# Layer norms of a two-layer encoder run tile by tile instead of side by side

## Chip, cores and metric

One core of a Trainium2 chip runs the whole program in one launch. The metric is the device time of one execution in microseconds (us), as the median over several runs. The engines are named as in the profile: PE is TensorE's matmul side and PEld its weight load, DVE is VectorE, ACT is ScalarE, POOL is GpSimd, SP is SyncE, which here only issues DMAs.

## What is computed

The reference is a float32 encoder of two layers over one sequence of 256 tokens and a model width of 1024. Each layer has four sub-blocks, each followed by a residual sum and a layer norm:

```
alpha = (2 * DEPTH) ** 0.25
x = LN(alpha*x + 0.5 * swiglu(x))          n = 0
x = LN(alpha*x + hybrid_mix(x))            n = 1
x = LN(alpha*x + cross_attention(x, mem))  n = 2
x = LN(alpha*x + 0.5 * swiglu(x))          n = 3
LN(v): (v - mean(v)) * rsqrt(mean((v - mean(v))**2) + 1e-5) * g + b
```

## The kernel before

**Tiles.** The 256 tokens are two token tiles (t = 0 and 1) of 128 partitions. X holds both, 128x1024 each. A matmul operand is split into a high and a low part in a reduced format, and three matmuls make one product (lines 412 to 414). So every weight block ("unit") is loaded to RAW by SP, copied by ACT to WH (the high part, line 917), and DVE subtracts to get WL (the low part, line 1232); ten units per two layers have this subtraction on POOL instead (line 1768). RAW, WH and WL are rings of three. The transposed activations XH and XL are made the same way: PE transposes X to PSUM (turn_x, line 481), ACT copies to XH, DVE subtracts to XL (both called turned).

**Order.** Each engine has its own program, written out by hand, and the engines meet only in semaphores. A loop runs over the two layers (l). After each sub-block comes boundary(l, n) on DVE and on ACT; the last norm of a layer (n = 3) is written out after ffn(l, 1).

**The norm on DVE.** norm_center(t) makes the residual sum of one tile with its row sum (line 1268), the negative mean (L1271), and XG, the centred row times the gain (L1274). It waits for the first token tile's product (y_half) at t = 0 and for the whole product (unit_used) at t = 1. ACT squares the centred row meanwhile and sums it (square, line 937). norm_scale(a, b) turns the sums of tiles a to b-1 into the variance (L1281), takes the reciprocal root by two integer steps and three Newton rounds of three instructions (rsqrt, lines 1246 to 1251; 11 instructions on 128 x (b-a) elements), and then makes the final X of each tile (L1285), which lets PE transpose it. link() around a small instruction makes the next one wait for its result.

**What stands behind it in the queues.** ACT's boundary is: square tile 0, [at n = 2 one weight copy], square tile 1, [at n = 0 the copy of unit U_DQ+1, at n = 0 and 1 the copy of one bank of keys or values, kv_out], then the copies to XH. At n = 3 ACT goes on with ffn of the next layer: one weight copy, then the copies to XH. PE at n = 0 transposes tile 0, multiplies it by U_DQ, transposes tile 1, then needs U_DQ+1, whose low part POOL makes at the end of its queue of table work. PE at n = 1 transposes both tiles and only starts the product with U_WQ when both are turned. At n = 2 and at the next layer's ffn it works on tile 0 before tile 1 is transposed. After the last norm SP writes X to memory, one DMA for each token tile as each is ready.

Of the kernel before, what the change touches and what calls it, by code (L numbers as in the profile page):

```python
# [69 lines left out]
TWO_PI = 6.2831850  # L70


DVE_LINKS, POOL_LINKS = 224, 111


def build(nc, x_in, mem_in, wg, wu, wd, ln_g, ln_b, w_in, w_out, wq, wkv, wo, par, const, out):
# [12 lines left out]
    with ctx:  # L89
# [1130 lines left out]
        def _(dve):  # L1220
# [4 lines left out]
            def link(ins):  # L1225

                count["n"] += 1
                ins.then_inc(dve_link.sem, 1)
                dve.wait_ge(dve_link.sem, dve_link.at(layer["l"], count["n"]))
# [4 lines left out]
            def split(l, u, j=0, half=False):  # L1234
                s = u % RING
                n = 1024 if half else 2048
                if u in (U_DQ + 2, U_K[3], U_WQ + 1, U_FFN[1] + 2):

                    dve.wait_ge(split_lo.sem, split_lo.at(l, u))
                dve.wait_ge(split_hi.sem, split_hi.at(l, u + 1 + 3 * j))  # L1240
                low(WL[s][:, 0:n], RAW[s][:, 0:n], WH[s][:, 0:n]).then_inc(split_lo.sem, 1)

            def rsqrt(dst, src, n, work, done=None):

                a, b = SM[:, work:work + n], SM[:, work + n:work + 2 * n]
                link(v.tensor_scalar(b.bitcast(I32), src.bitcast(I32), 1, None, ALU.logical_shift_right))
                link(v.tensor_scalar(dst.bitcast(I32), b.bitcast(I32), -1.0, 1597463007.0, ALU.mult, ALU.add))
                for i in range(3):
                    link(v.scalar_tensor_tensor(a, dst, -0.5, dst, ALU.mult, ALU.mult))
                    link(v.tensor_tensor(a, a, src, ALU.mult))  # L1250
                    ins = v.scalar_tensor_tensor(dst, a, 1.5, dst, ALU.add, ALU.mult)  # L1251
                    if i < 2 or done is None:
                        link(ins)
                    else:
                        ins.then_inc(done.sem, 1)
# [4 lines left out]
            def norm_center(l, n, t, last_unit):  # L1260

                c = (0.5 if n in (0, 3) else 1.0) / ALPHA
                if t == 0:
                    dve.wait_ge(y_half.sem, y_half.at(l, n + 1))
                    dve.wait_ge(gb_in.sem, gb_in.at(l, 32 * (n + 1)))
                else:
                    dve.wait_ge(unit_used.sem, unit_used.at(l, last_unit + 1))
                v.scalar_tensor_tensor(X[:, t, :], Y[:, t, :], c, X[:, t, :], ALU.mult, ALU.add,
                                       accum_out=SM[:, 16 + t:17 + t]).then_inc(ln_sum.sem, 1)
                dve.wait_ge(ln_sum.sem, ln_sum.at(l, TT * n + t + 1))  # L1270
                v.tensor_scalar(SM[:, 18 + t:19 + t], SM[:, 16 + t:17 + t], -1.0 / D, None, ALU.mult)\  # L1271
                    .then_inc(ln_mean.sem, 1)
                dve.wait_ge(ln_mean.sem, ln_mean.at(l, TT * n + t + 1))
                v.scalar_tensor_tensor(XG[:, t, :], X[:, t, :], SM[:, 18 + t:19 + t], LNGB[:, 0, :],  # L1274
                                       ALU.add, ALU.mult).then_inc(ln_center.sem, 1)

            def norm_scale(l, n, a, b):

                dve.wait_ge(ln_square.sem, ln_square.at(l, TT * n + b))
                var = SM[:, 20 + a:20 + b]  # L1280
                link(v.tensor_scalar(var, var, 1.0 / D, EPS / ALPHA ** 2, ALU.mult, ALU.add))  # L1281
                rsqrt(SM[:, 22 + a:22 + b], var, b - a, 48)
                dve.wait_ge(ln_center.sem, ln_center.at(l, TT * n + b))
                for t in range(a, b):
                    v.scalar_tensor_tensor(X[:, t, :], XG[:, t, :], SM[:, 22 + t:23 + t], LNGB[:, 1, :],  # L1285
                                           ALU.mult, ALU.add).then_inc(x_ready.sem, 1)

            def turned(l, n, t):
                for half in range(2):
                    dve.wait_ge(xT_hi.sem, xT_hi.at(l, 4 * n + 2 * t + half + 1))  # L1290
                    cs = slice(4 * half, 4 * half + 4)
                    low(XL[:, cs, t * P:t * P + P], PS[:, 4 + 2 * t + half, :].rearrange("p (c n) -> p c n", c=4),
                        XH[:, cs, t * P:t * P + P]).then_inc(xT_lo.sem, 1)

            def boundary(l, n, last_u):
                norm_center(l, n, 0, last_u)
                if n == 2:

                    norm_scale(l, n, 0, 1)
                norm_center(l, n, 1, last_u)  # L1300
                if n < 2:
                    norm_scale(l, n, 0, 2)
                turned(l, n + 1, 0)
                if n == 2:
                    norm_scale(l, n, 1, 2)
                turned(l, n + 1, 1)
                if n == 1:
                    split(l, U_WQ + 1)
                if n > 0:
                    split(l, U_WQ + 2 if n == 1 else U_FFN[1] + 2)  # L1310
# [5 lines left out]
            def ffn(l, s):  # L1316
                b = U_FFN[s]
                if s == 0:
                    split(l, b)
                    turned(l, 0, 0)  # L1320
                    split(l, b + 1)
                    turned(l, 0, 1)
                    split(l, b + 2)
                h_mul(l, 22 * s + 1, 0)
                split(l, b + 3)
                h_mul(l, 22 * s + 1, 1)
                split(l, b + 4)

                def step(j, jj, last):
                    dve.wait_ge(hT_hi.sem, hT_hi.at(l, jj + (11 * s + 1)))  # L1330
                    low(HL[:, :, :], PS[:, 6, :].rearrange("p (c n) -> p c n", c=2), HH[:, :, :])\
                        .then_inc(hT_lo.sem, 1)
                    split(l, b + 5, jj)
                    h_mul(l, jj * 2 + (22 * s + 3), 0)
                    h_mul(l, jj * 2 + (22 * s + 3), 1)
                    if not last:
                        split(l, b + 6, jj)
                        split(l, b + 7, jj)

                step(0, 0, False)  # L1340
                if s == 0:
                    prepare_first(l)
                step(1, 1, False)
                if s == 0:
                    prepare_phase(l)
                step(2, 2, False)
                if s == 0:
                    prepare_rest(l)
                with dve.Fori(3, BLOCKS - 2) as j:
                    step(j, j, False)  # L1350
                step(BLOCKS - 2, BLOCKS - 2, True)
                if s == 0:
                    split(l, U_K[0])
                dve.wait_ge(hT_hi.sem, hT_hi.at(l, 11 * s + BLOCKS))
                low(HL2[:, :, :], PS[:, 6, :].rearrange("p (c n) -> p c n", c=2), HH2[:, :, :]).then_inc(hT_lo.sem, 1)
# [372 lines left out]
            with dve.Fori(0, DEPTH) as l:  # L1728
                layer["l"] = l
                v.memset(CIN[:, :, 0:3], 0.0).then_inc(cin_zero.sem, 1)  # L1730
                ffn(l, 0)
                split(l, U_DQ)
                boundary(l, 0, U_FFN[0] + 32)
                mix(l)
                boundary(l, 1, U_WOUT[4])
                xattn(l)
                boundary(l, 2, U_WO + 4)
                ffn(l, 1)
                norm_center(l, 3, 0, U_FFN[1] + 32)
                norm_center(l, 3, 1, U_FFN[1] + 32)  # L1740
                norm_scale(l, 3, 0, 2)
            assert count["n"] == DVE_LINKS, count["n"]


# [229 lines left out]
```

## Time and profile before

| | |
|---|---|
| time, median of 3 runs | 1393.96 us (1392.83 to 1393.98) |
| span of the profiled execution, first to last instruction | 1392.3 us |
| median less that span | 1.7 us |
| PE busy / PEld busy | 91% / 75% |
| DVE / ACT / POOL busy | 61% / 42% / 31% |
| granted TensorE clock, mean | 0.949 |

The profiled execution has no time of its own beside the span; what lies around the span is taken as the 1.7 us by which the median exceeds it. A busy PE is not a PE at its peak, because matmuls are pipelined; gaps of PE are what is to be looked for. The norms lie, in layer 0, from about 207 us (n = 0), 414 us (n = 1), 488 us (n = 2) and 689 us (n = 3); in layer 1 from about 893, 1103, 1177 and 1379 us.

### The profile page before, as it was taken

Reading aid. Unit: us, or ns where it says so; the run is one execution under the profiler, and the core shown is the slowest. Engines: PE = TensorE matmul, PEld = TensorE weight load, DVE = VectorE, ACT = ScalarE, POOL = GpSimd, SP = SyncE. Lnnn points to the kernel's source line nnn. Section 1 sums busy time; section 2 is a strip of 40 time slices with the busy share of each in tenths; the row PEclk is TensorE's granted clock in tenths of the full one; section 3 lists DMA queues with packets and bytes.
Section 4 is the critical chain, followed back from the end, with each engine's and each line's share of the span. In section 5 each row is a group of like instructions: output and inputs, shape, how many; then the busy total and the mean of one; then the engine's idle time right before and its main releaser. Section 6 shows DMA issues by size and latency. Waiting matters only on the chain.

```text
span 1392.3 us, 18724 instructions
## 1 busy us (share of the span) xinstructions
PE 1267.4 (91%) x6160; PEld 1048.2 (75%) x6160; DVE 854.8 (61%) x1208; ACT 581.8 (42%) x651; POOL 432.1 (31%) x331
## 2 busy tenths in 40 slices
PE   5999997979968979999889999889797899799996
PEld 5878886857758868888768788777576687688885
DVE  4675555697885574444566655628978746644554
ACT  5433344423633443444354343444255334344432
POOL 0028886386040010000000588853851200100000
PEclk8999999998999989999989999989799899899999
DMA  7755553323334335555355555433233343455550
GB/s 271 263 177 194 181 182 113 129 93 106 136 121 152 121 131 202 191 193 187 123 205 193 186 194 192 152 121 118 94 122 121 121 152 122 151 181 190 194 188 31
DMA packets 151435, 219.13 MB, mean 157 GB/s; under 512 B 6721, under 2 KB 119489, under 8 KB 151105
## 3 DMA queue, kind: packets, MB, share of 16 engines
q1 hardware_dynamic: 148352, 205.61, 43.5%
q0 software_dynamic: 2736, 11.59, 2.3%
q10 hardware_dynamic: 272, 1.05, 0.2%
q8 instruction: 34, 0.56, 0.2%
q14 instruction: 41, 0.33, 0.1%
HBM read 217.17 MB, written 1.05 MB: 157 GB/s over the span
## 4 chain that ended last, share of the span: by engine, by line
PE 50%; POOL 22%; issue 14%; DVE 11%; ACT 1%; POOLq 1%; DMA 1%; DVEq 0%; SPq 0%; ACTq 0%
PE PS L412 15%; PE PS L413 15%; PE PS L414 15%; POOL ESN L1783 2%; POOL EC L1788 2%; POOL EC L1786 2%; DVE SM L1251 2%; POOL EF L1781 2%; POOL EF L1787 1%; POOL ESN L1790 1%; POOL ESN L1779 1%; POOL ESN L1782 1%; POOL EF L1789 1%; POOL ZX L1841 1%; DVE XG L1274 1%
## 5 line engine op out<-in xcount | busy, mean ns | idle before, releaser
L1232 DVE TENSOR_TENSOR WL<-RAW,WH 128x2048 fp32r<-128x2048 f32 (+1 forms) x188 | 427.2, 2273 | 277.8 <-ACT WH L917 274.6
L917 ACT ACTIVATE WH<-RAW 128x2048 fp32r<-128x2048 f32 (+1 forms) x198 | 371.1, 1877 | 185.6 <-PE PS L414 185.4
L412 PE MATMUL PS<-WH,XH 128*128 128x512 f32 x832 | 339.1, 408 | 36.9 <-DVE XL L1232 20.3
L413 PE MATMUL PS<-WL,XH 128*128 128x512 f32 x832 | 332.2, 399 | 0.0
L414 PE MATMUL PS<-WH,XL 128*128 128x512 f32 x832 | 331.8, 399 | 0.0
L412 PEld LDWEIGHTS PS<-WH,XH 128*128 128x128 f32 x832 | 161.2, 194 | 75.1 <-issue 24.4
L414 PEld LDWEIGHTS PS<-WH,XL 128*128 128x128 f32 x832 | 161.1, 194 | 35.1
L413 PEld LDWEIGHTS PS<-WL,XH 128*128 128x128 f32 x832 | 161.7, 194 | 32.3
L412 PE MATMUL PS<-WH,HH 128*128 128x512 f32 x352 | 137.5, 391 | 2.4 <-DVE HL L1232 2.4
L414 PE MATMUL PS<-WH,HL 128*128 128x512 f32 x352 | 137.0, 389 | 0.0
L413 PE MATMUL PS<-WL,HH 128*128 128x512 f32 x352 | 137.0, 389 | 0.0
L1768 POOL TENSOR_TENSOR WL<-RAW,WH 128x2048 fp32r<-128x2048 f32 x10 | 45.7, 4568 | 171.0 <-ACT WH L917 171.0
L917 ACT ACTIVATE HH<-PS 128x512 fp32r<-128x512 f32 x44 | 26.3, 598 | 157.5 <-PE PS L443 156.9
L1232 DVE TENSOR_TENSOR HL<-PS,HH 128x512 fp32r<-128x512 f32 x44 | 30.4, 691 | 83.0 <-ACT HH L917 82.8
L982 ACT ACTIVATE SG<-PS 128x256 f32<-128x256 f32 x88 | 33.8, 384 | 108.7 <-PE PS L414 108.7
L412 PEld LDWEIGHTS PS<-WH,HH 128*128 128x128 f32 x352 | 66.1, 188 | 16.8 <-issue 3.2
L414 PEld LDWEIGHTS PS<-WH,HL 128*128 128x128 f32 x352 | 66.1, 188 | 13.7
L413 PEld LDWEIGHTS PS<-WL,HH 128*128 128x128 f32 x352 | 66.1, 188 | 13.6
L1874 POOL DMA_DIRECT2D PAR<-in_params x2 | 1.1, 534 | 228.3 <-PE PS L414 228.3
L412 PE MATMUL PS<-XH,WH 128*128 128x256 f32 x224 | 66.3, 296 | 3.2 <-DVE XL L1232 3.2
L413 PE MATMUL PS<-XL,WH 128*128 128x256 f32 x224 | 64.8, 289 | 0.0
L414 PE MATMUL PS<-XH,WL 128*128 128x256 f32 x224 | 64.8, 289 | 0.0
(280 smaller groups left out, 1990.6 us busy)
## 6 DMA issues: line engine op xcount, KB each, us to landing
RAW<-in_ffn_w_gate SPq DMA_DIRECT2D x88, 512.0 KB, 3.7
RAW<-in_ffn_w_up SPq DMA_DIRECT2D x88, 512.0 KB, 4.7
RAW<-in_ffn_w_down SPq DMA_DIRECT2D x88, 512.0 KB, 3.9
RAW<-in_w_in SPq DMA_DIRECT2D x44, 512.0 KB, 4.1
RAW<-in_xattn_wkv SPq DMA_DIRECT2D x32, 512.0 KB, 4.1
RAW<-in_xattn_wq SPq DMA_DIRECT2D x16, 512.0 KB, 3.9
RAW<-in_w_out SPq DMA_DIRECT2D x12, 512.0 KB, 3.6
RAW<-in_xattn_wo SPq DMA_DIRECT2D x12, 512.0 KB, 4.0
```

Source lines behind the costliest of these rows:

```text
L412: nc.tensor.matmul(out_ap, sh, mh, start=first, stop=False)
L413: nc.tensor.matmul(out_ap, sh, ml, start=False, stop=False)
L414: return nc.tensor.matmul(out_ap, sl, mh, start=False, stop=last)
L917: return nc.scalar.activation(dst, src, ACT.Copy)
L982: nc.scalar.activation(SG[:, t, :], PS[:, 4 + t, 0:FB], ACT.Silu).then_inc(sg_done.sem, 1)
L1232: return v.tensor_tensor(dst, full, hi.bitcast(F32), ALU.subtract)
L1251: ins = v.scalar_tensor_tensor(dst, a, 1.5, dst, ALU.add, ALU.mult)
L1768: g.tensor_tensor(WL[s][:, :], RAW[s][:, :], WH[s][:, :].bitcast(F32), ALU.subtract)\
L1781: link(g.tensor_scalar(EF[:, :], s, MAGIC, MAGIC, ALU.add, ALU.subtract))
L1783: link(g.tensor_tensor(s, s, c, ALU.add))
L1786: link(g.tensor_scalar(c, s, 0.25, None, ALU.add))
L1788: link(g.tensor_tensor(c, c, EF[:, :], ALU.subtract))
```

## The change

The norms at n = 0, 1 and 3 get the order that n = 2 has: tile 0's sum, centring, variance, reciprocal root and scale are all done before tile 1's residual sum begins, and tile 1 gets a reciprocal root of its own. At n = 0 and 1 the low parts of tile 0's transposed activations (turned) are made between tile 1's centring and its scale. Nothing changes at n = 2. ACT's, PE's, POOL's and SP's programs stay as they are.

```diff
-DVE_LINKS, POOL_LINKS = 224, 111
+DVE_LINKS, POOL_LINKS = 260, 111
...
             def boundary(l, n, last_u):
                 norm_center(l, n, 0, last_u)
-                if n == 2:
-
-                    norm_scale(l, n, 0, 1)
+                norm_scale(l, n, 0, 1)
                 norm_center(l, n, 1, last_u)
-                if n < 2:
-                    norm_scale(l, n, 0, 2)
                 turned(l, n + 1, 0)
-                if n == 2:
-                    norm_scale(l, n, 1, 2)
+                norm_scale(l, n, 1, 2)
                 turned(l, n + 1, 1)
...
                 ffn(l, 1)
                 norm_center(l, 3, 0, U_FFN[1] + 32)
+                norm_scale(l, 3, 0, 1)
                 norm_center(l, 3, 1, U_FFN[1] + 32)
-                norm_scale(l, 3, 0, 2)
+                norm_scale(l, 3, 1, 2)
```

DVE_LINKS counts the linked instructions of one layer: 12 more for each of the three norms.

## Rows read from the trace of the kernel before

**Rows 1.** The page, part 4: shares of the chain that ended last.

```profile
PE 50%; POOL 22%; issue 14%; DVE 11%; ACT 1%; POOLq 1%; DMA 1%; DVEq 0%; SPq 0%; ACTq 0%
```

**Rows 2.** Timeline of DVE, last norm: start us, busy us, instruction, tiles.

```profile
1378.57 1.23 DVE L1268 SCALAR_TENSOR_TENSOR X<-PS,X 128x1024 f32<-128x1024 f32 x1 [4.24 <-PE PS L414]
...
1381.23 1.22 DVE L1268 SCALAR_TENSOR_TENSOR X<-PS,X 128x1024 f32<-128x1024 f32 x1
...
1383.95 0.17 DVE L1281 TENSOR_SCALAR SM<-SM 128x2 f32<-128x2 f32 x1
...
1386.32 2.48 DVE L1285 SCALAR_TENSOR_TENSOR X<-XG,SM,LNGB 128x1024 f32<-128x1024 f32 x2
```

**Rows 3.** Timeline of DVE and POOL, norm n = 2 of layer 0.

```profile
490.95 0.15 DVE L1281 TENSOR_SCALAR SM<-SM 128x1 f32<-128x1 f32 x1
...
493.03 4.50 POOL L1768 TENSOR_TENSOR WL<-RAW,WH 128x2048 fp32r<-128x2048 f32 x1 [64.84 <-ACT WH L917]
...
493.07 4.47 DVE L1251 SCALAR_TENSOR_TENSOR SM<-SM 128x1 f32<-128x1 f32 x1
...
498.78 1.22 DVE L1268 SCALAR_TENSOR_TENSOR X<-PS,X 128x1024 f32<-128x1024 f32 x1
...
503.19 0.14 DVE L1281 TENSOR_SCALAR SM<-SM 128x1 f32<-128x1 f32 x1
```

**Rows 4.** Timeline of SP's queue at the end: the two output DMAs.

```profile
1387.64 1.54 SPq L401 DMA_DIRECT2D out<-X  x2
```

**Rows 5.** Timeline of ACT, DVE and PE, n = 3 of layer 0.

```profile
697.28 1.91 ACT L917 ACTIVATE WH<-RAW 128x2048 fp32r<-128x2048 f32 x1
...
700.19 2.29 DVE L1232 TENSOR_TENSOR WL<-RAW,WH 128x2048 fp32r<-128x2048 f32 x1
...
702.40 1.28 DVE L1232 TENSOR_TENSOR XL<-PS,XH 128x512 fp32r<-128x512 f32 x2
...
703.93 0.79 PE L412 MATMUL PS<-WH,XH 128*128 128x512 f32 x1 [3.67 <-DVE XL L1232]
```

**Rows 6.** Timeline of POOL, DVE, ACT and PE, n = 1 of layer 0.

```profile
412.94 4.62 POOL L1768 TENSOR_TENSOR WL<-RAW,WH 128x2048 fp32r<-128x2048 f32 x1 [13.34 <-ACT WH L917]
...
415.04 3.60 DVE L1274 SCALAR_TENSOR_TENSOR XG<-X,SM,LNGB 128x1024 f32<-128x1024 f32 x1
...
421.96 0.60 ACT L917 ACTIVATE KT<-PS 128x512 f32<-128x512 f32 x1 [0.71 <-PE PS L414]
...
423.92 2.48 DVE L1285 SCALAR_TENSOR_TENSOR X<-XG,SM,LNGB 128x1024 f32<-128x1024 f32 x2
...
429.87 0.58 PE L412 MATMUL PS<-XH,WH 128*128 128x256 f32 x1 [1.59 <-DVE XL L1232]
```

**Rows 7.** Timeline of DVE, POOL and PE, n = 0 of layer 0.

```profile
207.31 1.22 DVE L1268 SCALAR_TENSOR_TENSOR X<-PS,X 128x1024 f32<-128x1024 f32 x1
...
216.36 1.07 POOL L1789 TENSOR_SCALAR EF<-ESN 128x256 f32<-128x256 f32 x1 [0.19 <-POOL EC L1788]
...
216.42 3.08 DVE L1285 SCALAR_TENSOR_TENSOR X<-XG,SM,LNGB 128x1024 f32<-128x1024 f32 x2
...
218.38 1.59 POOL L1804 TENSOR_TENSOR CP<-PAR,CUR 128x256 f32<-128x256 f32 x1
...
225.20 4.54 POOL L1768 TENSOR_TENSOR WL<-RAW,WH 128x2048 fp32r<-128x2048 f32 x1
...
225.81 1.04 PE L481 MATMUL PS<-kst,X 128*128 128x128 f32 x8
...
229.79 0.50 PE L412 MATMUL PS<-WH,XH 128*128 128x512 f32 x1 [2.94 <-POOL WL L1768]
```

**Rows 8.** Windows: length, busy us (count) of PE, PEld, DVE, ACT, POOL; clock; DMA.

```profile
220.96:225.00 4.04, 4.04 (x10) 3.17 (x11) 0.00 (x0) 0.00 (x0) 3.31 (x5) 0.50 0.00 0
...
229.79:233.00 3.21, 3.21 (x14) 2.66 (x15) 2.43 (x2) 3.15 (x2) 0.00 (x0) 1.00 0.60 185
```

**Rows 9.** Timeline of DVE in the mixing stage behind n = 0.

```profile
254.61 0.47 DVE L1397 TENSOR_SCALAR ROW<-PS,PAR 4x256 f32<-4x256 f32 x1 [11.11 <-PE PS L731]
```

## The prediction

> **What bounds the kernel now.** I read first the page's chain of work that ended last. Half of it is matmuls, a fifth POOL, a tenth DVE [rows 1]: no one engine bounds the kernel, the stages hand over to each other. So the question is local: at each of the eight norms, which event does PE wait for last, and does that event move? The timeline of each norm answers it, and the reader should look there for PE's bracket, the idle time with its releaser. Three kinds appear. At n = 1 PE stands until tile 1 is turned as well [rows 6]. At the n = 3 of layer 0 it stands until DVE has turned tile 0 [rows 5]; at the last norm there is nothing left but DVE and the output DMA [rows 2, 4]. At n = 0 PE gets tile 0, multiplies, transposes tile 1, and then waits 2.94 us for the weight subtraction on POOL [rows 7]: there tile 1 is ready with time to spare. The norm n = 2 already has the new order and shows what it costs [rows 3].
>
> **The DVE chain itself.** In the quiet last norm, tile 0's sum to tile 1's sum takes 2.66 us, tile 1's sum to the variance 2.72, variance to first scale 2.37, the two scales 2.48 together: 10.23 us from 1378.57 to 1388.80 [rows 2]. In the new order each tile runs sum and centring 2.72, a root of width one, and a scale. The root: at n = 2 the eleven instructions before the last start within 2.12 us (490.95 to 493.07); with the last one of some 0.19 us the scale can start 2.31 us after the variance [rows 3]. Width one against two saves next to nothing. One scale is 1.24. Laid end to end: 2.72 + 2.31 + 1.21 = 6.24 us until tile 1's sum begins, and twice that, 12.48, to the end. The new norm is 2.25 us longer on DVE. What it gives is tile 0 earlier by 2.37 + 2.72 + 2.66 + 1.24 - 6.27 = 2.7 us. Tile 1's sum and its square on ACT begin 6.24 - 2.66 = 3.58 us later than now. Everything follows from who stands behind which of the two.
>
> **Last norm (once).** Only tile 1's end counts. DVE +2.25. Tile 0's DMA is issued first [rows 4] and is now long out of the way when tile 1's starts, which can give back a few tenths, as the issue itself takes 0.77 us for each. I take +2.2, bounds +1.9 and +2.3.
>
> **n = 3 of layer 0 (once).** Tile 0's early X does not help: behind it on DVE stand tile 1's whole chain, the low part of the next weight unit, and only then tile 0's XL. On ACT the weight copy of 697.28 stands behind the square of tile 1, so it comes 3.58 later and ends at 697.28 + 3.58 + 1.91 = 702.77. DVE is free for the subtraction at 700.19 + 2.25 = 702.44, so ACT is what comes last: subtraction at 702.8 instead of 700.19, XL and PE +2.6 behind it [rows 5]. Bounds: +2.25 if the start-up of ACT's new loop round overlaps, +3.5 if PE, having idled longer, also stays at the low clock longer. Tile 1 is hidden: PE then has tile 0's matmuls to do. I take +2.6.
>
> **n = 1 (twice).** PE needs both tiles, so nothing hides. POOL's weight subtraction holds DVE's first XG until 418.64 [rows 6], in both orders. New: root and scale to 418.65 + 2.31 + 1.21 = 422.17, when tile 1's sum begins. At n = 2 the variance of tile 1 starts 4.41 us after its sum, because DVE's turned of tile 0 stands between and waits for ACT [rows 3]; here ACT has kv_out's copy in front of XH too, 0.5 of its 0.60 [rows 6]. So 427.1, then the root and a scale of 1.28: tile 1 ready at 430.7, against 423.92 + 2.48 = 426.40 now. That is +4.3. The way on to PE's first matmul (3.47 us now, 426.40 to 429.87) stays. Bounds: +3.9, since tile 1's transposes no longer queue behind tile 0's; +5.3, if the longer idle adds a low-clock stretch. I take +4.3.
>
> **n = 0 (twice).** Tile 0: with POOL working, sum to first scale took 9.11 us here [rows 7] against 7.75 in the quiet [rows 2], 1.36 lost in meetings with POOL. Allowing 1.3 again, tile 0 is scaled at 207.31 + 6.24 + 1.3 = 214.9. Then tile 1's sum and centring; ACT squares, copies a weight unit (1.91, as in [rows 5]) that now stands behind this later square, copies keys, and only then XH: tile 0 is turned at 214.9 + 4.41 + 0.5 + 1.9 = 221.7, some 0.8 later than now. PE's product with U_DQ moves by that and still ends before POOL's unit. DVE's second root starts at 221.7 and wants to scale tile 1 at 224.0, or up to 225 if POOL's scale_c instructions get in between. And at 225.20 POOL begins the 4.54 us subtraction [rows 7], or up to 1 us sooner, since its product of 218.38, now 1.59 us behind the two scales, no longer meets them together. It is a race within a microsecond. At n = 2 one sees who loses: a root instruction that takes 0.16 us otherwise lasted 4.47 because it came 0.04 us after POOL's subtraction had begun [rows 3].
> If POOL wins, rest of root and scale come after it: POOL 224.7 to 229.2, scale to 230.7, PE transposes tile 1 (1.04 at full clock [rows 7], estimated 1.5 at less) until 232.2, and starts on U_DQ+1 there instead of at 229.79: +2.4. PE has then idled longer than the 2.94 us after which it now keeps the 2.4 GHz level (clock 1.00, 14 matmuls in 3.21 us); from 220.96, after the norm's own wait, it ran 10 matmuls in 4.04 us at the 1.2 GHz level (0.50) [rows 8]. A like stretch costs 4.04 - 10 x 0.229 = 1.75. I take half of it, +0.8: in all +3.2, bounds +1.2 (POOL early, clock kept) and +4.9 (POOL as now, whole low stretch). If DVE wins, POOL loses at most one scale and may have been earlier: +0.5, bounds -1.0 and +1.0.
> Does it arrive? Behind n = 0 PE has no gap, and DVE waits 11.11 us for PE at 254.61 [rows 9], so the delay goes on whole.
> I choose POOL first, because it needs only one of several DVE instructions to come late.
>
> **A rule weighed.** The two scales at 216.42 took 3.08 us where POOL's instruction had begun 0.06 us before and ran until 217.43 [rows 7]; in the quiet they took 2.48 [rows 2], so the meetings there cost 0.6 in all. The Trainium skill, SBUF — State Buffer, section "SBUF: two separate sides", states that DVE with two SBUF inputs and GpSimd hold their shared port pair as an exclusive lock, whoever starts second being blocked for the other's whole instruction. By it the first scale alone would have lost 1.0, which this row does not show, while the 4.47 us row does. By the rule n = 0 would come out some 0.4 later each time, 20.6 in place of 19.8 in the sum below.
>
> **The sum.** 2 x 3.2 + 2 x 4.3 + 2.6 + 2.2 = 19.8 us. The span of 1392.3 becomes 1412.1; with the 1.7 around it, and so against the median, 1413.8. n = 2 adds nothing. The 36 added small instructions a layer are in these terms.
>
> **Rivals.**
> DVE wins the race at n = 0: 2 x 0.5 + 8.6 + 4.8 = 14.4, time 1408.4. For it: the times are a microsecond apart. Against: the roots meet POOL's products all along.
> The second root is hidden everywhere, as it is at n = 2, where PE multiplies tile 0 meanwhile: 1394. It decides if PE has tile 0's work to do while tile 1 is in its root. At n = 1 PE's order forbids it, at the last norm there is no work.
> Faster: tile 0's head start of 2.7 us reaches PE at the n = 3 of layer 0, so that gate and up products start at 701.2, and nothing else moves: 1393.96 - 2.7 = 1391.3. It decides if XL of tile 0 is made before tile 1's chain ends; DVE's queue puts it behind.
> Worse: low-clock stretches in full at both n = 0 and n = 1, and POOL's unit late: 9.8 + 10.6 + 3.5 + 2.3 = 26.2, time 1420.
>
> **From cases to numbers.** POOL first 0.56, DVE first 0.30, worse 0.06, hidden 0.04, head start 0.04. The likeliest gives 1413.8. Its lower bounds, 2.4 + 7.8 + 2.25 + 1.9 = 14.3, give 1408.3; the DVE-first case's are -2 + 7.8 + 4.15 = 9.95, 1403.9. The range 1405 to 1418.5 leaves out hidden, head start, most of worse and the tips of the two others, under 2 in 10. A measurement of this kernel tells about 0.2%, 2.8 us, from no change: slower 0.92, same 0.04, faster 0.04.
>
> **What would show it.** At the end DVE's last scale ends 12.5 us after the norm's first sum, not 10.2. At n = 1 PE's first U_WQ matmul starts 19.1 us after the first XG, not 14.8 (415.04 to 429.87). At the n = 3 of layer 0 ACT's weight copy ends after DVE is free. At n = 0 a root or scale instruction of DVE lasts about 4 us beside POOL's subtraction, and PE's bracket names DVE's X, not POOL's WL. The prediction is wrong if that long instruction is absent, if PE's start at n = 1 moves by under 3 us, or if the stage behind n = 0 swallows the delay before 254.61.

## The result and the profile after

The changed kernel takes 1409.26 us (1408.24 to 1409.9, 4 runs) against 1393.97 us (1392.83 to 1396.77, 4 runs): a ratio of 1.0105, with a 95% interval of 1.0091 to 1.0119, or +15 us. The profiled spans are 1408.1 and 1392.3 us, a difference of 15.8 us.

The page of the changed kernel, parts 1 and 4, the latter beside [rows 1]:

```profile
span 1408.1 us, 18874 instructions
...
PE 1266.0 (90%) x6160; PEld 1047.7 (74%) x6160; DVE 867.0 (62%) x1280; ACT 580.8 (41%) x651; POOL 435.4 (31%) x331
...
PE 49%; POOL 22%; issue 14%; DVE 11%; ACT 2%; POOLq 1%; DMA 1%; SPq 0%; DVEq 0%; ACTq 0%
```

The page hardly differs; no share in it tells where 15.8 us went. What tells it is the start of the first residual sum (L1268) of each norm, read from the timeline of DVE in both traces. It cuts the span into nine pieces:

| from ... to | before, us | after, us | difference |
|---|---|---|---|
| start to n = 0, layer 0 | 207.31 | 207.04 | -0.27 |
| n = 0 to n = 1, layer 0 | 206.28 | 209.27 | +2.99 |
| n = 1 to n = 2, layer 0 | 74.64 | 78.73 | +4.09 |
| n = 2 to n = 3, layer 0 | 200.96 | 200.93 | -0.03 |
| n = 3 to n = 0 of layer 1 | 203.73 | 207.06 | +3.33 |
| n = 0 to n = 1, layer 1 | 209.89 | 209.17 | -0.72 |
| n = 1 to n = 2, layer 1 | 74.61 | 78.92 | +4.31 |
| n = 2 to n = 3, layer 1 | 201.15 | 201.05 | -0.10 |
| n = 3 to the end | 13.73 | 15.93 | +2.20 |

n = 1 costs nearly the same in both layers, the pieces behind n = 3 and at the end are longer by 3.3 and 2.2 us, and n = 2 costs nothing. The piece behind n = 0 is +3.0 in one layer and -0.7 in the other, with the same code in both: that pair needs an explanation of its own.

**The last norm.** Timeline of DVE, to be held against [rows 2], and of SP's queue, against [rows 4]:

```profile
1392.17 1.23 DVE L1268 SCALAR_TENSOR_TENSOR X<-PS,X 128x1024 f32<-128x1024 f32 x1 [4.24 <-PE PS L414]
...
1403.45 1.28 DVE L1285 SCALAR_TENSOR_TENSOR X<-XG,SM,LNGB 128x1024 f32<-128x1024 f32 x1
```
```profile
1398.53 6.59 SPq L401 DMA_DIRECT2D out<-X  x2
```

The last scale ends at 1404.73, 12.56 us after the first sum; it was 10.23.

**n = 1 of layer 0.** The first sum in the kernel before, then timelines of DVE and PE of the changed one, against [rows 6]:

```profile
413.59 1.23 DVE L1268 SCALAR_TENSOR_TENSOR X<-PS,X 128x1024 f32<-128x1024 f32 x1 [2.04 <-PE PS L414]
```
```profile
416.31 1.23 DVE L1268 SCALAR_TENSOR_TENSOR X<-PS,X 128x1024 f32<-128x1024 f32 x1 [2.07 <-PE PS L414]
...
417.77 3.61 DVE L1274 SCALAR_TENSOR_TENSOR XG<-X,SM,LNGB 128x1024 f32<-128x1024 f32 x1
...
424.81 1.22 DVE L1268 SCALAR_TENSOR_TENSOR X<-PS,X 128x1024 f32<-128x1024 f32 x1
...
432.01 1.28 DVE L1285 SCALAR_TENSOR_TENSOR X<-XG,SM,LNGB 128x1024 f32<-128x1024 f32 x1
```
```profile
433.35 1.97 PE L481 MATMUL PS<-kst,X 128*128 128x128 f32 x8 [7.30 <-DVE X L1285]
436.91 0.58 PE L412 MATMUL PS<-XH,WH 128*128 128x256 f32 x1 [1.59 <-DVE XL L1232]
```

PE stands 7.30 us for tile 1's X. From the first XG to PE's first product with U_WQ it is 436.91 - 417.77 = 19.14 us, and was 14.83; from the first sum it is 20.60 us, and was 16.28. In layer 1 it is 20.60 us too, and was 16.01.

**n = 3 of layer 0.** The kernel before on DVE, then timelines of DVE, ACT and PE of the changed one, against [rows 5]:

```profile
689.19 1.22 DVE L1268 SCALAR_TENSOR_TENSOR X<-PS,X 128x1024 f32<-128x1024 f32 x1 [4.24 <-PE PS L414]
...
696.95 2.48 DVE L1285 SCALAR_TENSOR_TENSOR X<-XG,SM,LNGB 128x1024 f32<-128x1024 f32 x2
700.10 0.07 DVE L1730 MEMSET CIN<- 128x12 f32 x1 [0.68 <-issue]
```
```profile
695.97 1.23 DVE L1268 SCALAR_TENSOR_TENSOR X<-PS,X 128x1024 f32<-128x1024 f32 x1 [4.24 <-PE PS L414]
...
707.26 1.28 DVE L1285 SCALAR_TENSOR_TENSOR X<-XG,SM,LNGB 128x1024 f32<-128x1024 f32 x1
710.43 0.07 DVE L1725 MEMSET CIN<- 128x12 f32 x1 [1.89 <-issue]
710.52 2.29 DVE L1232 TENSOR_TENSOR WL<-RAW,WH 128x2048 fp32r<-128x2048 f32 x1
```
```profile
707.65 1.91 ACT L917 ACTIVATE WH<-RAW 128x2048 fp32r<-128x2048 f32 x1
```
```profile
714.25 0.79 PE L412 MATMUL PS<-WH,XH 128*128 128x512 f32 x1 [10.32 <-DVE XL L1232]
```

ACT's copy ends at 709.56; DVE, whose scale ended at 708.54, begins its next instruction only at 710.43. The bracket says "issue": DVE waited for nothing that the profile shows. PE's product starts 18.28 us after the first sum, and started 14.74 after it before.

**n = 0 of layer 0.** Timelines of DVE, POOL and PE, against [rows 7], and windows against [rows 8]:

```profile
207.04 1.22 DVE L1268 SCALAR_TENSOR_TENSOR X<-PS,X 128x1024 f32<-128x1024 f32 x1
...
214.15 1.22 DVE L1268 SCALAR_TENSOR_TENSOR X<-PS,X 128x1024 f32<-128x1024 f32 x1
...
220.84 0.14 DVE L1281 TENSOR_SCALAR SM<-SM 128x1 f32<-128x1 f32 x1
...
223.09 0.68 DVE L1251 SCALAR_TENSOR_TENSOR SM<-SM 128x1 f32<-128x1 f32 x1
...
224.58 1.29 DVE L1285 SCALAR_TENSOR_TENSOR X<-XG,SM,LNGB 128x1024 f32<-128x1024 f32 x1
```
```profile
224.77 5.49 POOL L1764 TENSOR_TENSOR WL<-RAW,WH 128x2048 fp32r<-128x2048 f32 x1
```
```profile
225.93 1.09 PE L481 MATMUL PS<-kst,X 128*128 128x128 f32 x8
230.31 0.50 PE L412 MATMUL PS<-WH,XH 128*128 128x512 f32 x1 [3.29 <-POOL WL L1764]
```
```profile
230.31:233.30 2.99, 2.99 (x10) 2.45 (x11) 2.43 (x2) 2.79 (x2) 0.00 (x0) 0.75 0.59 168
233.30:236.00 2.70, 2.70 (x9) 2.11 (x9) 0.00 (x0) 0.00 (x0) 0.00 (x0) 0.65 1.08 380
```

The scale starts 0.19 us ahead of POOL's subtraction, which then lasts 5.49 us instead of 4.54. PE still waits for POOL's WL, not for X. It resumes 23.27 us after the first sum, and resumed after 22.48 before: +0.8. What comes on top is TensorE's clock: it falls to the 1.2 GHz level soon after PE has resumed (eight matmuls of 0.63 us from 231.81 on, against 0.39 before), where in the kernel before it stayed at 1.00. Together they make +2.4: the row of [rows 9] starts at 256.75 here, 49.71 us after the first sum, and was at 47.30.

In layer 1 PE waits 3.29 us as well and the clock stays at 1.00 in this kernel, while it fell in the kernel before. Windows, first of the kernel before, then of this one:

```profile
915.38:921.50 6.12, 6.12 (x14) 4.79 (x15) 2.43 (x2) 3.36 (x2) 0.00 (x0) 0.50 0.83 276
```
```profile
926.29:932.00 5.71, 5.71 (x25) 4.75 (x26) 2.43 (x2) 2.79 (x2) 0.00 (x0) 1.00 0.81 267
```

So PE comes out of this stretch 2.1 us sooner than before, counted from the first sum. At the ends of the two pieces +2.4 and -2.1 have become +3.0 and -0.7. The difference arises later in the mixing stage, in code that the change doesn't touch, partly by other stretches of low clock (in layer 0, 1.0 us of it near 405 us, where matmuls of 0.39 us last 0.63).

### The profile page after: what moved, and what is told of

It is laid out like the page before. It is cut to its first block, busy times and chain, and to the rows that moved or that the text cites. A ratio compares the mean times of both kernels' runs of the same rounds, so it can differ in the third digit from the quotient of the medians.

```text
span 1408.1 us, 18874 instructions
## 1 busy us (share of the span) xinstructions
PE 1266.0 (90%) x6160; PEld 1047.7 (74%) x6160; DVE 867.0 (62%) x1280; ACT 580.8 (41%) x651; POOL 435.4 (31%) x331
## 4 chain that ended last, share of the span: by engine, by line
PE 49%; POOL 22%; issue 14%; DVE 11%; ACT 2%; POOLq 1%; DMA 1%; SPq 0%; DVEq 0%; ACTq 0%
PE PS L412 15%; PE PS L413 15%; PE PS L414 15%; POOL ESN L1779 2%; POOL EC L1784 2%; POOL EF L1783 2%; POOL EC L1782 2%; POOL EF L1777 2%; POOL EF L1785 1%; POOL ESN L1786 1%; POOL ESN L1775 1%; POOL ESN L1778 1%; POOL ZX L1837 1%; DVE SM L1250 1%; DVE SM L1251 1%
## 5 line engine op out<-in xcount | busy, mean ns | idle before, releaser
L414 PEld LDWEIGHTS PS<-WH,HL 128*128 128x128 f32 x352 | 66.1, 188 | 13.8
```

Source lines behind the costliest of these rows:

```text
L414: return nc.tensor.matmul(out_ap, sl, mh, start=False, stop=last)
```

## The experiments

Each ratio is to the kernel before, timed beside it on the same chip.

### One norm at a time

`n0_only`, `n1_only` and `n3_only` are the kernel before with the new order at one norm alone. At n = 0 and n = 1 the edit is this one, with the other conditions on n turned in the same way; at n = 3 it is the part of the change behind ffn(l, 1):

```diff
             def boundary(l, n, last_u):
+                apart = n in (2, 0)        # n1: (2, 1)
...
-                if n == 2:
+                if apart:
```

> Only the norm n = 0 runs tile by tile; n = 1 and n = 3 as before. Theory (the costs are local and add up): PE resumes on U_DQ+1 0.8 us later in each layer, counted from the norm's first sum, because POOL's subtraction was held by tile 1's scale; that alone is +1.6 us in all. What else n = 0 showed in the changed kernel, +2.2 in layer 0 and -1.5 in layer 1, is the TensorE clock granted after PE's wait, which may fall either way: total from -1.5 to +5, near +2. Rival (the second root itself delays PE in the mixing stage): +3 in each layer, +6.

> Only the norm n = 1 runs tile by tile. Theory (nothing hides there, because PE needs both tiles): +4.1 to +4.3 us in each layer, +8.4 in all, with PE's first matmul on U_WQ 20.4 us after the norm's first sum in place of 16.3. Rival (part of it came from the stages ahead, which were shifted by n = 0): under +6.

> Only the last norm of each layer (n = 3) runs tile by tile. Theory (second root exposed on DVE, and behind it in layer 0 the loop's restart): +3.3 us between the layers and +2.2 at the end, +5.5 in all. Rival (the restart gap of DVE, 1.9 us in place of 0.7, was chance): +4.5 in all, with that gap at 0.7 again.

| new order at | ratio | 95% interval | us |
|---|---|---|---|
| n = 0 (12 runs) | 1.0011 | 0.9998 to 1.0023 | +1.5 |
| n = 1 (6 runs) | 1.0051 | 1.0035 to 1.0068 | +7.1 |
| n = 3 (10 runs) | 1.0037 | 1.0021 to 1.0053 | +5.2 |
| all three | 1.0105 | 1.0091 to 1.0119 | +14.7 |

The last column is the ratio less one, times 1395 us. The three add up to 13.8, as near to the whole change as the intervals allow. n = 1 is half of it. n = 0, which was 6.4 of my sum, is 1.5, with an interval from -0.3 to +3.2 us that excludes the 6 us of the rival. In `n3_only` DVE's idle time between the layers is 1.78 us, so the 1.89 of the changed kernel was no chance.

In `n3_only` n = 0 is untouched, and yet PE, after a wait of 2.84 us there, ran at the low clock. Timeline of PE, and its window:

```profile
229.82 0.80 PE L412 MATMUL PS<-WH,XH 128*128 128x512 f32 x1 [2.84 <-POOL WL L1769]
```
```profile
229.82:232.82 3.00, 3.00 (x7) 2.44 (x8) 2.43 (x2) 3.00 (x2) 0.00 (x0) 0.50 0.55 171
```

In [rows 8] the same code after a wait of 2.94 us ran at 1.00. So the clock behind this wait goes either way without the change. Seven of the profiles have PE waiting there for POOL, in both layers. With the old order at n = 0 the clock fell behind 4 of 6 waits (of 2.73 to 3.04 us) and 14, 14, 14 and 8 matmuls ran slow; with the new one it fell behind 7 of 8 (of 3.29 or 3.30 us), 8 slow matmuls each time. Eight slow matmuls cost 1.6 us and fourteen 2.9 (+2.4 and -2.1 above, less the 0.8 of the wait). That is 8.3 slow matmuls a wait in the old order against 7.0 in the new: no price of the new order shows in it, though so few waits can't exclude a small one.

### The race at n = 0, lost on purpose

Three small linked instructions of DVE stand before tile 1's scale at n = 0, so that the scale comes behind POOL's start. They compute on a spare column.

```diff
                 rsqrt(SM[:, 22 + a:22 + b], var, b - a, 48)
+                if n == 0 and a == 1:
+                    for i in range(3):
+                        link(v.tensor_scalar(SM[:, 48:49], SM[:, 48:49], 1.0, None, ALU.mult))
```

> The changed kernel with three more small linked instructions on DVE (0.57 us) ahead of tile 1's scale at n = 0. In the changed kernel that scale starts 0.19 us before POOL's weight subtraction. Theory (an exclusive meeting between the two engines, won narrowly): now POOL starts first, the scale waits out its 4.5 us, tile 1 is ready some 5 us later, PE resumes 1.5 to 2 us later per layer and may lose up to 1.6 more to the clock: +3 to +7 us over the changed kernel, of which the added instructions themselves are 1.1. Rival (no exclusive meeting; tile 1 is early enough anyway): at most +1.

1416.27 us, ratio 1.0152 (1.0134 to 1.0169). Against the changed kernel's 1.0105 that is +6.6 us (3.1 either way), for 0.6 us of added instructions in each layer. Timelines of DVE, POOL and PE:

```profile
224.84 0.53 DVE L1285 TENSOR_SCALAR SM<-SM 128x1 f32<-128x1 f32 x3
225.41 5.22 DVE L1288 SCALAR_TENSOR_TENSOR X<-XG,SM,LNGB 128x1024 f32<-128x1024 f32 x1
```
```profile
225.03 4.52 POOL L1767 TENSOR_TENSOR WL<-RAW,WH 128x2048 fp32r<-128x2048 f32 x1
```
```profile
230.69 1.97 PE L481 MATMUL PS<-kst,X 128*128 128x128 f32 x8 [4.46 <-DVE X L1288]
232.31 0.78 PE L412 MATMUL PS<-WH,XH 128*128 128x512 f32 x1
```

This is the case that I had held likeliest, row for row: a DVE instruction drawn out beside POOL's subtraction, and PE's bracket naming X. The pieces behind n = 0 are 3.2 and 3.5 us longer than in the changed kernel. PE starts on U_DQ+1 25.03 us after the first sum, 2.55 later than in the kernel before, where I had put 2.4, and 7 and 8 matmuls behind it run slow in the two layers. The mechanism is real and its price about right; the changed kernel misses it by 0.19 us.

### POOL's subtractions off the boundaries

At n = 0, PE waits for POOL in both orders. Here DVE makes U_DQ+1's low part itself, behind the two low parts of tile 0 (the norm n calls turned with n + 1), and POOL no longer does; first in the kernel before, then in the changed one:

```diff
             def turned(l, n, t):
+                if n == 1 and t == 0:
+                    split(l, U_DQ + 1)
...
-                split(l, U_DQ + 1)
```

> The kernel before, with the low part of unit U_DQ+1 made by DVE between tile 0's and tile 1's turned (where DVE sat idle 6.4 us) and not by POOL. Theory (at n = 0 PE waits for POOL's subtraction, nothing else): PE goes from tile 1's transposes straight to U_DQ+1, 2.9 us earlier in each layer, -5.8 us, and with the wait gone the clock stays up more often: -5 to -9. Rival (DVE's subtraction meets POOL's table work and delays it and DVE as much): -2 to 0.

> The changed kernel with the same move of U_DQ+1 to DVE. Theory (at n = 0 POOL's wait was the cover of tile 1's second root): DVE's queue is now XL of tile 0, subtraction, root, scale, so tile 1 is ready near 20.5 us after the norm's first sum and PE starts U_DQ+1 near 21.7, some 1.6 us earlier than in the changed kernel but 2 us later than with the move alone. Against the changed kernel -3 to -5; against the move alone +17 to +18, more than the +14.7 that the change costs with POOL's unit in place. Rival (the second root is free at n = 0 in any case): +14 against the move alone.

The kernel before becomes 1383.1 us, ratio 0.9925 (0.9908 to 0.9942), about 10.5 us faster. Timeline of PE:

```profile
225.74 1.04 PE L481 MATMUL PS<-kst,X 128*128 128x128 f32 x8
226.53 0.47 PE L412 MATMUL PS<-WH,XH 128*128 128x512 f32 x1
```

There is no wait between the two, U_DQ+1 starts 19.29 us after the first sum instead of 22.48, and the clock stays at 1.00 behind it. Twice 3.2 us are 6.4, and in layer 1, where the kernel before had its 14 slow matmuls, PE gains 2.9 more. The pieces behind n = 0 end 1.8 us shorter in layer 0, where 2.2 us of the gain are lost again near 398 us to matmuls at the low clock, and 7.0 in layer 1. The pieces behind n = 1, whose code is untouched, are 1.2 and 2.2 us shorter too; their cause wasn't traced, and with them the gain is above the 5 to 9 us expected.

With the new order it is 1407.48 us, ratio 1.0092 (1.007 to 1.0115). Against the changed kernel this is no difference (-1.8 us, 3.7 either way), where -3 to -5 was expected. The distance between the two orders has grown to 0.0167, or 23 us (3.9 either way), more than expected. Timelines of DVE and PE of this kernel:

```profile
227.33 1.28 DVE L1285 SCALAR_TENSOR_TENSOR X<-XG,SM,LNGB 128x1024 f32<-128x1024 f32 x1
```
```profile
228.67 1.32 PE L481 MATMUL PS<-kst,X 128*128 128x128 f32 x8 [1.98 <-DVE X L1285]
```

PE now waits for tile 1's X and starts U_DQ+1 22.07 us after the first sum (22.28 in layer 1) instead of 19.29: 2.8 us for the new order, where it was 0.8. So the new order was cheap at n = 0 because POOL's late subtraction hid most of the second root. With that cover gone the root lies in the open, and 7 and 6 slow matmuls behind the wait come on top, where there were none. A further part of the 23 us lies behind n = 1: the pieces there differ by 5.2 and 6.6 us instead of 4.1 and 4.3, because they are held against the two that came out short without a traced cause.

> The kernel before with U_DQ+1 and U_FFN[1]+1 made on DVE, the second at n = 2 between tile 1's scale and its turned. Theory (at n = 2 a root instruction stands 4.3 us behind POOL's subtraction, and PE behind it): tile 0 is ready 4.3 us earlier in each layer and DVE's 2.3 us subtraction lies beside PE's work on tile 0: -8.6 beyond the first move, -14 in all. Rival (PE then waits for the subtraction before its second unit): half of that, -10 in all.

> As the run with two units on DVE, and U_WQ too, ahead of the norm n = 1, where POOL's subtraction now holds tile 0's XG for 2.3 us. DVE can start it some 1.4 us before the norm has to wait for it to end. Theory: -0.9 us a layer, -1.8 beyond the two. Rival: the sums start late by as much as the meeting cost, 0.

These two go on from the faster kernel and move U_FFN[1]+1 (at n = 2), and then U_WQ (ahead of n = 1), from POOL to DVE as well: 1375.99 us, ratio 0.9872 (0.9851 to 0.9892), and 1373.63 us, ratio 0.9849 (0.9827 to 0.9871). Beyond the first move that is -7.4 us for the second, where -8.6 was expected, and -3.2 for the third (4.2 either way), where it was -1.8. The first one ends the stall of [rows 3]: tile 1's sum at n = 2 starts 6.26 us after tile 0's instead of 10.55. The second one ends the long XG of [rows 6], and tile 1's sum at n = 1 starts 2.64 us after tile 0's instead of 4.97. But tile 0's sum comes later by 3.2 and 3.9 us in the two layers, and the pieces on either side of it together are only 0.1 and 0.6 us shorter. The intervals overlap as well, so it is not shown that the third move pays; all three together are 21 us faster than the kernel before, 36 faster than the changed one.

### The change undone where it had always stood

n = 2 gets the side by side order, in the kernel with two units moved:

```diff
-                if n == 2:
-                    norm_scale(l, n, 0, 1)
                 norm_center(l, n, 1, last_u)
-                if n < 2:
-                    norm_scale(l, n, 0, 2)
+                norm_scale(l, n, 0, 2)
...
                 if n == 2:
-                    norm_scale(l, n, 1, 2)
```

> Starts from the kernel before with U_DQ+1's and U_FFN[1]+1's low parts on DVE (0.987 of the kernel before), and gives n = 2 the side by side order as well, the one norm that has always run tile by tile. This is the change undone at the place where it could pay: at n = 2 PE works on tile 0 before it needs tile 1. Theory (tile by tile brings tile 0 forward by 2.7 us where the consumer takes tiles one at a time and the second root is covered): without it PE's first matmul behind n = 2 comes 1.3 to 2.7 us later in each layer, +2.6 to +5 us against the kernel it starts from, a ratio of about 0.989 to 0.991. Rival (DVE is what comes last here too, and 2.3 us less of it per norm wins, as at n = 1 and n = 3): -2 to -4 us, a ratio of about 0.984 to 0.986.

1383.49 us, ratio 0.9917 (0.9902 to 0.9931), against 0.9872: +6 us, 3.5 either way. The two pieces behind n = 2 are 4.6 and 3.9 us longer. So at this norm tile by tile is the better order; that it is so by more than the 1.3 to 2.7 us a layer that I had put is shown by the rows, not by the times. Timeline of DVE, first of this kernel, then of the one it starts from:

```profile
486.31 1.22 DVE L1268 SCALAR_TENSOR_TENSOR X<-PS,X 128x1024 f32<-128x1024 f32 x1 [1.29 <-PE PS L414]
...
491.65 1.23 DVE L1268 SCALAR_TENSOR_TENSOR X<-PS,X 128x1024 f32<-128x1024 f32 x1 [2.60 <-PE PS L414]
...
496.76 2.48 DVE L1285 SCALAR_TENSOR_TENSOR X<-XG,SM,LNGB 128x1024 f32<-128x1024 f32 x2
```
```profile
484.45 1.23 DVE L1268 SCALAR_TENSOR_TENSOR X<-PS,X 128x1024 f32<-128x1024 f32 x1 [1.30 <-PE PS L414]
...
489.50 1.29 DVE L1285 SCALAR_TENSOR_TENSOR X<-XG,SM,LNGB 128x1024 f32<-128x1024 f32 x1
490.71 1.22 DVE L1268 SCALAR_TENSOR_TENSOR X<-PS,X 128x1024 f32<-128x1024 f32 x1
```

Tile 1's half of the product isn't there when DVE wants it: side by side, DVE waits 2.60 us for PE with tile 0 centred and unscaled. Tile 0's scale starts 10.45 us after the first sum instead of 5.05, and PE's next product comes 15.36 us after it (501.67) instead of 10.99 (495.44). Tile by tile spends on tile 0's root the time that DVE would wait anyway. In the kernel before, the stall of [rows 3] eats this gain: PE's next product comes 15.28 us after the first sum there, hardly sooner than side by side here.

### How much of the second root is on the path

In the changed kernel, tile 1's root at n = 1 and n = 3 leaves out two of three Newton rounds:

```diff
-                rsqrt(SM[:, 22 + a:22 + b], var, b - a, 48)
+                rsqrt(SM[:, 22 + a:22 + b], var, b - a, 48, rounds=1 if n in (1, 3) and a == 1 else 3)
```

> The changed kernel, but tile 1's reciprocal root at n = 1 and at n = 3 leaves out two of its three Newton rounds: six small DVE instructions of about 0.195 us each, 1.17 us less at four places; the norm's result is a little coarser for that tile. It measures by itself whether the second root is on the path there. Theory (second root exposed in full at n = 1 in both layers and at both n = 3): -4.7 us against the changed kernel, a ratio of about 1.007 where the changed kernel has 1.0105; the segments behind n = 1, behind n = 3 of layer 0 and the last norm are each 1.2 us shorter. Rival (at n = 3 of layer 0 something other than DVE comes last, ACT's copy as predicted): that segment stays, -3.5 us. Rival (the second root is hidden behind other work): 0.

1405.28 us, ratio 1.0084 (1.0066 to 1.0103). Against the changed kernel that is -2.9 us, 3.2 either way: the ratio alone separates neither -3.5 from -4.7 nor either from nothing. The spans differ by 4.6 us and the rows decide. At n = 1 PE's product starts 19.41 us after the first sum instead of 20.60, in both layers: all of the 1.17. At n = 3 of layer 0 (timeline of DVE):

```profile
708.97 0.07 DVE L1725 MEMSET CIN<- 128x12 f32 x1 [1.79 <-issue]
709.37 2.29 DVE L1232 TENSOR_TENSOR WL<-RAW,WH 128x2048 fp32r<-128x2048 f32 x1 [0.34 <-ACT WH L917]
```

Counted from tile 1's sum, PE's product comes after 11.10 us instead of 12.03, 0.93 less; DVE now waits 0.34 us for ACT's copy. ACT's copy was thus the next thing behind DVE, some 0.9 us behind it, and not the last one. (The pieces themselves are 0.7 and 0.9 us shorter behind n = 1, 1.8 behind n = 3 and 0.9 at the end.)

### The idle time at the loop's end

> The changed kernel, but at n = 3 tile 0's scale is taken out of its place and stands with tile 1's at the end: two roots of width one, as in the changed kernel, then two scales in a row, as in the kernel before. DVE's work in the norm is the same. It asks where DVE's idle time between the last scale of layer 0 and the first instruction of layer 1 comes from: 0.58 to 0.89 us in every kernel with two scales at the end, 1.78 to 1.93 us in every kernel with one. Theory (the restart of the loop takes a fixed 3.1 to 3.4 us from the start of the last scales, and a long instruction that is still running covers it): the idle time is 0.6 to 0.9 us, and PE's first matmul behind n = 3 starts about 17.1 us after the norm's first sum, not 18.3; one place in the kernel, so -1.2 us, a ratio of about 1.0095 to 1.010. The last norm's last scale still ends 12.5 us after its first sum. Rival (the idle time belongs to the longer program, with 12 more linked instructions at the loop's end): it stays at 1.8 to 1.9 us, and PE's start stays at 18.3.

The edit leaves all the work in the norm and only moves tile 0's scale at n = 3:

```diff
+                if n == 3 and a == 0:
+                    return
                 dve.wait_ge(ln_center.sem, ln_center.at(l, TT * n + b))
-                for t in range(a, b):
+                for t in range(0 if n == 3 else a, b):
```

Timelines of DVE and PE:

```profile
699.20 1.22 DVE L1268 SCALAR_TENSOR_TENSOR X<-PS,X 128x1024 f32<-128x1024 f32 x1 [4.24 <-PE PS L414]
...
709.37 2.48 DVE L1287 SCALAR_TENSOR_TENSOR X<-XG,SM,LNGB 128x1024 f32<-128x1024 f32 x2
712.67 0.07 DVE L1727 MEMSET CIN<- 128x12 f32 x1 [0.82 <-issue]
```
```profile
716.50 0.79 PE L412 MATMUL PS<-WH,XH 128*128 128x512 f32 x1 [3.81 <-DVE XL L1232]
```

The idle time falls from 1.89 to 0.82 us and PE starts 17.30 us after the first sum instead of 18.28. From the start of the last scales to the first instruction of the next round it is 3.30 us here, 3.17 in the changed kernel and 3.15 in the kernel before: the same within 0.15, whether one scale or two cover it. The rival falls, since the program is as long as the changed one. The time, 1410.1 us, ratio 1.011 (1.0088 to 1.0131), shows nothing of 1 us: the two pieces behind n = 0, whose code is untouched, came out 2.1 and 1.4 us longer at the same mean clock (0.91 and 0.90, against 0.90 and 0.90), for a reason that wasn't traced, while the piece behind n = 3 was 1.9 shorter.

## Why the prediction was right, and where it was not

**Right: direction and place.** The stages hand over to each other, so a longer DVE chain shows wherever PE stands behind it. No piece of the span gave the delay back; the delay behind n = 0 arrived whole at the row of [rows 9]. The head start of tile 0 brought PE's transposes forward (at n = 0 to 7.25 us after the first sum, from 10.58) and no product.

**Last norm, +2.2:** measured +2.20, the last scale 12.56 us after the first sum against 12.48 worked out.

**n = 1, +4.3 each:** measured +4.3 from the norm's first sum to PE's first product in layer 0 (20.60 less 16.28) and +4.6 in layer 1 (20.60 less 16.01), and +4.1 and +4.3 in the pieces. Alone it gave +7.1, whose interval holds twice 4.3. The short root confirms the reason: what is cut from the second root comes off one for one.

**n = 3 of layer 0, +2.6:** measured +3.5. The mechanism was right, the term was too small, and the thing that I named as last was the wrong one. I took DVE's idle time between the layers as it stood and let ACT's copy decide. But that idle time was what remained of a restart of 3.1 to 3.4 us after two scales had covered 2.48 of it; one scale covers 1.28. DVE's own term is 2.25 + 1.2 = 3.45. The experiment with the scales last shows this.

**n = 0, +3.2 each:** this is the step that failed, and by the prediction's own sign it failed outright: it was to be wrong if no root or scale of DVE lasted about 4 us beside POOL's subtraction, and in the changed kernel none does. I chose "POOL first", "because it needs only one of several DVE instructions to come late"; DVE came first, and the step is worth 0.8 each before the clock (1.5 for both, measured alone). The working was off by tenths on both sides: tile 0's chain lost 0.87 us to POOL and not 1.3 (214.15 - 207.04 - 6.24), which made tile 0's low parts ready 0.6 us sooner, at 13.80 us after the first sum instead of 14.4; the second root then lost 1.4 us, more than I gave it. A race decided by 0.19 us can't be called from rows with errors of half a microsecond, so a spread over both cases was right and 0.56 for one was a guess. Once decided it is no coin, though: the scale is ahead by 0.19 us in layer 0, by 0.18 in layer 1 (920.57 against 920.75), and by 0.19 with n = 0 changed alone.

The sum by measured terms is 2 x 0.8 + 2 x 4.2 + 3.5 + 2.2 = 15.7 us, against 15.8 between the spans. The clock behind n = 0 nearly cancels between these two profiles: over the whole pieces layer 0 lost 2.2 us beyond the 0.8, and layer 1 won 1.5. The time is thus that of my rival "DVE wins the race", 14.4 with 0.5 at n = 0; the likeliest case's 19.8 was too high by twice 2.4 at n = 0 and too low by 0.9 at n = 3. It lay in the range because the range covered both cases of the race; the case that I held likeliest didn't happen.

**The rule weighed.** Two rows of this study show what a whole subtraction does. A scale that starts 0.38 us behind POOL's TENSOR_TENSOR lasts 5.22 us instead of 1.28, and POOL's subtraction that starts 0.19 us behind the scale lasts 5.49 instead of 4.54, longer by nearly what was left of the scale, 1.10. The Trainium skill, SBUF — State Buffer, section "SBUF: two separate sides", says that whichever starts first gets the shared pair for its whole instruction; both rows agree with that rule to 0.2 us. The row at 216.42 in [rows 7], where POOL's instruction was a TENSOR_SCALAR with one tensor input, still shows less than the rule would have it: the first of the two scales lost 0.14 us where POOL's instruction had 1.01 left to run.

## What to carry to other kernels

Handling tiles one after the other brings the first forward and sets the last back. It paid where the consumer takes tiles one at a time and the second tile's input arrives late (n = 2: worth some 4 us in each layer, once POOL's subtraction is out of the way). Where the extra work is covered, it cost little (n = 0: 0.8 us); where the consumer needs both tiles, it cost the whole of the extra chain (n = 1: 4.3 us). Ask of each place what hides the added work, since a cover such as POOL's subtraction at n = 0 vanishes when somebody mends it: the largest gain in this kernel, 21 us, came from taking POOL's weight subtractions off the norms, and the first of these moves makes the change dearer, 23 us instead of 15.

## What the runs showed of the hardware

The end of a hardware loop on DVE has a restart of 3.06 to 3.37 us, counted from the start of the last scales to the first instruction of the next round, in all thirteen kernels; an instruction that still runs covers it. The idle time left was 0.58 to 0.89 us in the eight kernels with two scales there, and 1.78 to 1.93 us in the five with one.

Behind a wait of PE of 2.8 to 3.3 us, TensorE's clock either kept the 2.4 GHz level or fell to 1.2 GHz for some microseconds, in the same code and after waits equal to 0.1 us: in the changed kernel, after 3.29 us in both layers, it fell in layer 0 and stayed in layer 1, and in the kernel before it was the other way round. Each time it had stood at 2.4 GHz when PE began to wait. What tips it was not found.
